# Gathered rows moved within the sample's attention, and a second gate load asked for later

## The reference

```python
x = layer_norm(x, emb_ln_g, emb_ln_b)
h = x @ w_in                                    # fourier, q, k, v, two gates
f_branch = fourier_mix(f_in) @ w_fo             # FFT over tokens and within groups of 64
a_branch = window_attention(q, k, v, sink) @ w_ao   # blocks of 128, neighbours, 8 heads, 2 kv heads
merged = gates[..., :D] * f_branch + gates[..., D:] * a_branch
x = layer_norm(alpha * x + merged @ w_out)
cm = peer(x, pq, pkeys, pu, pv)                 # 8 heads x 16 of 16384 experts per token
ple = sigmoid(x @ ple_wg) * (p @ ple_wp)
out = layer_norm(alpha * x + cm + ple)
# peer, per token: 128 experts chosen by product keys, gate = softmax of their scores
act = gelu(xc . u[eidx]);  cm = sum over k of gate_k * act_k * v[eidx_k]
```

## Time and profile before

| | |
|---|---|
| median of 3 runs | 3372.86 us (3372.45 to 3387.92) |
| the profiled execution | 3368.09 us |
| its span, first to last instruction | 3366.2 us |
| PE busy | 3206.8 us, 95% |
| PE weight loads busy | 2632.9 us, 78% |
| VectorE busy | 1968.2 us, 58% |
| GpSimd busy | 1866.5 us, 55% |
| ScalarE busy | 1024.1 us, 30% |
| moved by DMA | 988.38 MB, mean 294 GB/s |
| mean granted clock of TensorE | 0.982 of full |

### The profile page before, as it was taken

The page is one execution under the profiler, slowest core; times in us unless marked ns, Lnnn a source line. Parts: engine busy times, 40 slices in busy tenths (PEclk is TensorE's granted clock), DMA queues, the critical chain, the costliest instruction groups (busy, mean ns, idle before and its releaser), DMA issues.

```text
span 3366.2 us, 40493 instructions
## 1 busy us (share of the span) xinstructions
PE 3206.8 (95%) x14740; PEld 2632.9 (78%) x14740; DVE 1968.2 (58%) x3363; ACT 1024.1 (30%) x1427; POOL 1866.5 (55%) x1430
## 2 busy tenths in 40 slices
PE   7999899999999997899999999999997999999996
PEld 6677787888888886578778888888886888888885
DVE  3511315994100000854648997888885678887888
ACT  2432222333322221410102333444443223322231
POOL 3034344655544432665474332777777688888872
PEclk9999899999999999999999999999998999999998
DMA  6268678777777876598789998999999999999995
GB/s 243 91 213 274 225 243 301 242 241 240 243 238 244 252 242 226 149 347 336 257 320 350 317 326 293 371 393 394 393 394 409 353 340 340 343 354 333 346 349 180
DMA packets 322538, 988.38 MB, mean 294 GB/s; under 512 B 46896, under 2 KB 80176, under 8 KB 310960
## 3 DMA queue, kind: packets, MB, share of 16 engines
q1 hardware_dynamic: 226960, 708.80, 60.4%
q0 software_dynamic: 91264, 272.96, 22.6%
q10 hardware_dynamic: 4128, 4.19, 0.4%
HBM read 737.28 MB, written 248.51 MB: 293 GB/s over the span
## 4 chain that ended last, share of the span: by engine, by line
PE 55%; POOL 19%; issue 17%; DMA 3%; DVE 3%; another core or an unknown queue 2%; DVEq 1%; SPq 0%; ACT 0%; POOLq 0%; ACTq 0%
PE ps L1280 17%; PE ps L1282 17%; PE ps L1281 17%; POOL value L831 7%; POOL v_row L848 7%; POOL w_lo L797 4%; PE ps L1585 3%; POOL u_lo L797 1%; DMA v_row<-in_v_rows,row_i 1%; DVE acc L936 1%; DMA pair<-pair_dram 1%; DMA pair_dram<-w_lo 0%; PE ps L1503 0%; DMA u_lo<-lo_dram 0%
## 5 line engine op out<-in xcount | busy, mean ns | idle before, releaser
L1280 PE MATMUL ps<-xt_hi,w_hi 128*128 128x512 f32 (+1 forms) x2424 | 988.6, 408 | 32.0 <-issue 20.5
L848 POOL DMA_INDIRECT v_row<-in_v_rows,row_i x512 | 675.3, 1319 | 521.7 <-DVE acc L936 405.0
L1281 PE MATMUL ps<-xt_lo,w_hi 128*128 128x512 f32 (+1 forms) x2424 | 940.4, 388 | 0.0
L936 DVE SCALAR_TENSOR_TENSOR acc<-v_row,share,acc 128x1024 f32<-128x1024 f32 x512 | 658.0, 1285 | 249.7 <-DMA v_row<-in_v_rows,row_i 194.8
L1282 PE MATMUL ps<-xt_hi,u_lo 128*128 128x512 f32 x2048 | 801.4, 391 | 0.0
L831 POOL DMA_INDIRECT value<-act_dram,value_i x512 | 645.6, 1261 | 226.0 <-issue 155.7
L797 POOL TENSOR_TENSOR u_lo<-u_raw,w_hi 128x512 fp32r<-128x512 f32 x256 | 359.9, 1428 | 346.1 <-ACT w_hi L683 338.8
L1280 PEld LDWEIGHTS ps<-xt_hi,w_hi 128*128 128x128 f32 x2424 | 459.9, 190 | 110.7 <-issue 26.0
L1281 PEld LDWEIGHTS ps<-xt_lo,w_hi 128*128 128x128 f32 x2424 | 459.9, 190 | 71.2 <-issue 0.2
L1282 PEld LDWEIGHTS ps<-xt_hi,u_lo 128*128 128x128 f32 x2048 | 385.5, 188 | 82.4
L702 ACT ACTIVATE act_t<-ps 128x512 f32<-128x512 f32 x256 | 153.1, 598 | 971.9 <-PE ps L1282 888.2
(11 more groups left out here) (210 smaller groups left out, 4086.0 us busy)
## 6 DMA issues: line engine op xcount, KB each, us to landing
u_raw<-in_u_t SPq DMA_DIRECT2D x256, 512.0 KB
pair<-pair_dram SPq DMA_DIRECT2D x69, 1024.0 KB
lo_dram<-u_lo SPq DMA_DIRECT2D x128, 512.0 KB, 5.3
act_dram<-act_t SPq DMA_DIRECT2D x256, 256.0 KB
u_lo<-lo_dram SPq DMA_DIRECT2D x128, 512.0 KB
u_raw<-in_v_rows SPq DMA_DIRECT2D x128, 512.0 KB
w_raw<-in_weights SPq DMA_DIRECT2D x69, 512.0 KB, 5.2
pair_dram<-w_hi SPq DMA_DIRECT2D x69, 512.0 KB, 5.7
```

The lines of the kernel that those rows point to most:

```text
L848: pool.indirect_dma_start(out=v_row[:, i % ROWS_DEEP, :], out_offset=None, in_=v_rows, in_offset=bass.IndirectOffsetOnAxis(ap=row_i[:, tt, ...
L936: dve.scalar_tensor_tensor(out=there, in0=v_row[:, i % ROWS_DEEP, :], scalar=share[:, tt, k:k + 1], in1=there, op0=ALU.mult, op1=ALU.add). ...
L1280: pe.matmul(where, lh, rh, start=first, stop=False)
L1281: pe.matmul(where, lh, rl, start=False, stop=False)
```

## The change

Three things are changed. The rows added in the sample's attention: none in units 0 and 1, four in each of units 2 to 7 (24 in all, as before). The call with START_ROWS, which added nothing, is gone. And ScalarE asks for gate group 0 after the activation of tile 121 as before, and for group 1 after that of tile 126.

```diff
--- before.py
+++ after.py
@@ -74,7 +74,7 @@
 
 GATHERS = NT * HK
 ROWS_DEEP = 4
-START_ROWS, UNIT_ROWS = 0, 3
+UNIT_ROWS, ROWS_FROM = 4, 2
 GAP_ROWS, GAPS = 1, 10
 BATCH_ROWS, LAST_ROWS = 2, 18
 FIRST_VALUES = 18
@@ -85,7 +85,7 @@
 def rows_before(j):
 
     tiles = min(j, OUT_AT) - MERGE_AT + max(0, j - QUERY_AT)
-    return START_ROWS + UNITS * UNIT_ROWS + 2 * tiles
+    return (UNITS - ROWS_FROM) * UNIT_ROWS + 2 * tiles
 
 
 def reloaded(n):
@@ -134,7 +134,7 @@
     return ROWS_CHOICE + BATCH_ROWS * max(0, batch - 1)
 
 
-assert SEQS == 2 and FIRST_LOADS_AT + DEEP < EXPERT_TILES and EXPERT_TILES % DEEP == 0
+assert SEQS == 2 and FIRST_LOADS_AT + 5 < EXPERT_TILES and EXPERT_TILES % DEEP == 0
 
 
 def nth_norm(s, which):
@@ -750,11 +750,11 @@
                     if n == EXPERT_TILES - 1:
                         split_v(0)
                     gelu(n)
-                    if n == FIRST_LOADS_AT:
+                    if n in (FIRST_LOADS_AT, FIRST_LOADS_AT + 5):
                         act.wait_ge(g_stored, 16 * PIECES)
-                        for group in range(2):
-                            rows = slice(group * G_GROUP, (group + 1) * G_GROUP)
-                            act.dma_start(g_in[group][:], g_dram[:, :, rows, :].rearrange("c j i t -> j c i t")).then_inc(g_back[group], 16)
+                        group = (n - FIRST_LOADS_AT) // 5
+                        rows = slice(group * G_GROUP, (group + 1) * G_GROUP)
+                        act.dma_start(g_in[group][:], g_dram[:, :, rows, :].rearrange("c j i t -> j c i t")).then_inc(g_back[group], 16)
                     if n == NORM_PROMPT_AT:
                         deviation(4, prompt_norms)
                         prompt_norms += 1
@@ -1099,8 +1099,6 @@
                                           ps[rows, 3, :].rearrange("p (a b q) -> p a b q", a=2, b=2)[:, :, half, :],
                                           o_hi0[rows, 2 * g:2 * g + 2, cols_of(blk)].bitcast(F32), ALU.subtract).then_inc(o_lo_made, 1)
 
-                if s:
-                    add_rows(START_ROWS)
                 dve.wait_ge(mix_in, 32 * (s + 1))
                 scores(0)
                 dve.wait_ge(v_ps, s + 1)
@@ -1112,7 +1110,7 @@
                         outputs_lo(u - 1)
                     if u + 1 < UNITS:
                         scores(u + 1)
-                    if s:
+                    if s and u >= ROWS_FROM:
                         add_rows(UNIT_ROWS)
                     if u % 2 and s == 0:
                         c = u // 2
```

## The result

The changed kernel took 3395.49 us (median of 14 runs, 3383.31 to 3409.8); the kernel before, in 14 runs on the same chip, 3382.32 (3368.69 to 3396.76). The ratio is 1.0041, with a 95% interval of 1.0024 to 1.0058: about 14 us slower by the ratio, where a gain of 0.9 was forecast.

The account below looks back on a forecast made before the run. TensorE, busy 95% of 3366.2 us, was taken as the bound, VectorE setting its pace in attention units 2 to 5. +5.1 and -5.8 summed to -0.7 us, 3367.4 profiled, 3372 as median; range 3357 to 3381.

Parts of the forecast that it names:

- Edit 1, +5.1: Sample's attention: moving the row additions to units 2 to 7 makes the attention end 5.1 us later.
- 5.52 + 0.93 - 1.3: Sample's attention: 5.52 us later in units 2, 3, 4 and 6, 0.93 in unit 5, 1.3 earlier in unit 1.
- the fourth row: Sample's attention: a fourth gathered row per unit arrives in time, by 0.9 us with three key tiles.
- Edit 2, -5.8: Gate stage: asking for the second gate group after tile 126 wins 5.8 us net.
- 8.5: End of gate stage: the down stage can begin 8.5 us earlier, at 2626.9 instead of 2635.36.
- 2.67 for a slow start: Start of down stage: TensorE, having idled 8 us, pays 2.67 us for a slow start.
- A: Gate stage: loads keep up once TensorE moves, all 20.9 us are won, total 3357; chance 0.18.
- four short waits: Gate stage: queue 1 needs 6.7 us a tile, so TensorE waits 1 to 2 before tiles 123, 125, 126, 127.
- C: Gate stage: the second issue still blocks, at tile 126, so moving it brings nothing, total 3378; chance 0.08.
- D: Attention: added rows fall into waits set by TensorE or ScalarE, -1.3 in place of +5.1, total 3366; chance 0.17.
- B: Attention: with four row buffers VectorE waits for fourth rows in units 3 to 7, 5.7 us more, total 3378; chance 0.12.
- theory G: Whole kernel, from the experiments: while GpSimd issues gathers without rest for over some 10 us, TensorE runs slow until it rests.

Follow-up runs that it names:

- paced burst: Kernel before, with the 18 first value gathers asked for three at a time behind each of six weight tiles: 3359.55 us, 0.9947.
- where the gathers rest: 39 value gathers spread in threes ahead of the attention, in the kernel before with moved rows only (3364.88 us, 0.9987) and in the changed kernel (3366.11, 0.9983).
- the rows alone: Kernel before with only the moved rows (none in units 0 and 1, four in 2 to 7), gate loads as before: 3400.9 us, 1.0058.
- the early burst: Kernel before, with the 18 first value gathers allowed behind the third tile of v weights instead of the tenth: 3377.91 us, 0.998.
- The runs with rests: Changed kernel with 18 first value gathers in threes behind six weight tiles (0.9964), or 39 in threes over 13 points ahead of the attention (0.9983).
- the combined runs: Kernel before with second gate group after tile 126, plus 18 value gathers in threes (3353.76 us, 0.9949) or 39 in threes (3356.05, 0.9948).
- the double burst: Kernel before, with 36 instead of 18 value gathers issued ahead of the rows, the same number in all: 3392.43 us, 1.0064.

## Why the prediction was wrong

**What bounds the kernel.** Right that PE's idle time is what can be won, and that 20.46 us hung on the second issue of line 757. Wrong in passing over the 20.03 us in the attention with the words "that the diff doesn't touch". It is a cost of the same GpSimd queue that edit 1 rearranges: with the burst paced it fell to 3.23. I read its releaser by name, where the "remote" wait of 22.93 on VectorE and the unbroken issues on GpSimd stood beside it.

**Edit 1, +5.1: the step that failed.** Its arithmetic holds. Unit 2's normalisation came early (units 1 and 2 are 8.97 us apart instead of 10.53), the units then are 11.6 us apart, and where the gathers rest the attention is longer by 5.9 and 4.9 us. But the sum "5.52 + 0.93 - 1.3" counted only VectorE. The step asked of the fourth row whether it arrives in time, and never what its issue does to others. From unit 1 to unit 7 the attention grew by 12.9 us (72.43 for 59.49) and by 11.6 in the rows alone, of which 6 to 7 are PE's lateness behind the issues.

I had also written that PE works "without a break" through the merges. In the changed kernel it doesn't: here is PE, with GpSimd issuing until 1548.5, and ScalarE's wait that ended 2.8 us later:

```profile
1542.15 0.40 PE L1279 MATMUL ps<-o_lo,pair 128*128 128x512 f32 x1 [0.92 <-issue]
1542.84 0.39 PE L1280 MATMUL ps<-o_hi,pair 128*128 128x512 f32 x1 [0.30 <-issue]
1543.54 0.40 PE L1278 MATMUL ps<-o_hi,pair 128*128 128x512 f32 x1 [0.31 <-issue]
```

```profile
1551.35 0.60 ACT L636 ACTIVATE sig<-ps 128x512 f32<-128x512 f32 x1 [15.75 <-remote]
```

One matmul each 0.7 us, where these run at 0.23. But that this belongs to edit 1 isn't shown. From the attention's last output to the first product of the merged branches (tile `m`) PE took 139.7 us before (1425.8 to 1565.5) and 159.6 in the changed kernel, yet 140.3 with the rows alone, and 149.2 with the early burst and the rows of before. So of the 19.6 us, give or take 6, that edit 1 cost in time, the attention shows 11.6, and the rest isn't placed.

The runs with rests give a rougher price. With the gathers paced ahead of the attention the edit cost 5 (0.9964 for 0.9949), with rests in it too 12 (0.9983 for 0.9948), each give or take 9. Both allow VectorE's 5 alone, but the second, in which the attention has its rests, allows the 19.6 as well. So it is the profiles of the attention, not these times, that show the loss shrinking where GpSimd rests (5.9 and 4.9 for 12.9 and 11.6).

**Edit 2, -5.8.** Right in mechanism, and timed at -7, give or take 6. In the profiles, from the last gate matmul to the first down matmul (starts), the six kernels with the old order and the values took 70.6 to 73.6 us, the six with the new order 64.5 to 67.3: 6.3 less by the means, where I had 8.5. The down stage itself took 3.7 more (mean 710.2 for 706.5), where I had 2.67 for a slow start. So the profiles leave 2.6 us of it, the time says 7, give or take 6, and the combined runs show nothing that can be told from 0: the size stays open.

By the Trainium skill, page Trainium Kernel Development and Optimization, section Key Constraints, spreading issues "only saves the sequencer's issue time". The runs agree as far as they go: 18 us of issue vanished from ScalarE's queue and at most 13 of time.

**Rivals.** A (-20.9 in the gate stage) is out: the four short waits came back where queue 1 said. C is out: 395 ns. D is out: VectorE's units are 11.6 apart. B, the slower one, had the right sign and the wrong mechanism: rows wait for their buffers, but what comes late is PE's result. Its price, +5.7, was near the lateness in the attention (6 to 7) by luck.

**The range.** Of the 23 us between the forecast 3372 and 3395.49, 9.5 are in the base: the kernel before, 3372.86 in three runs, has a median of 3382.32 in 14. The other 14 are the change's. The range held nothing for a stretch in which another engine's habits change, and 0.86 on "within 0.5%" was right only because the loss, 0.41%, stays below it.

**The better kernel.** Before with the paced burst is 0.5% faster than before (0.9947) and, by the two ratios, 0.9% faster than the changed one (1.0041), with 18 gathers placed elsewhere and nothing removed.

## What to carry to other kernels

When a change fills the rests of an engine that issues indirect DMAs, ask what the slower pace was worth to TensorE, and look for waits laid to "remote" whose producer's row ends long before. Issue such gathers a few at a time behind events of the stream, not as one burst. And a large wait beside the change deserves its own reading, even where the diff doesn't name its line.

## What the runs showed of the hardware that I had not expected

GpSimd's indirect DMAs, one per 1.25 us without a rest, slowed TensorE here to a third or less. With the first burst it began some 13 to 20 us after the first of them. In the kernel before the results were there as the last gather was issued, elsewhere up to 5.7 us behind it, and in the double burst some came through in between (VectorE's at 1360.25, with GpSimd issuing until 1375.63). Ten us without a rest (1319.38 to 1329.1 with the paced burst) did nothing, and rests of up to 2 us behind each three prevented it. The onset, from PE's rows of the kernel with the early burst, whose GpSimd has issued since 1284.85:

```profile
1303.95 0.39 PE L1282 MATMUL ps<-xt_hi,pair 128*128 128x512 f32 x1
1304.72 0.39 PE L1280 MATMUL ps<-xt_hi,pair 128*128 128x512 f32 x1 [0.38 <-issue]
1306.14 0.39 PE L1281 MATMUL ps<-xt_lo,pair 128*128 128x512 f32 x1 [1.04 <-issue]
1307.55 0.40 PE L1282 MATMUL ps<-xt_hi,pair 128*128 128x512 f32 x1 [1.02 <-issue]
...
1310.37 0.59 PE L1281 MATMUL ps<-xt_lo,pair 128*128 128x512 f32 x1 [1.71 <-issue]
```

```profile
1304.00:1306.00 2.00, 0.73 (x3) 0.33 (x2) 0.00 (x0) 0.00 (x0) 1.63 (x2) 1.00 0.02 1
```

These matmuls follow one another at 0.23 us until 1303.95, then with gaps of up to 1.71 that are laid to nothing but "issue". It isn't the clock: in the stretch shown (columns as above) the granted clock is 1.00, the full 2.4 GHz, the first three matmuls behind gaps last 0.39 to 0.40 us as before them, and only the one at 1310.37 is longer, after PE has stood more than half the time. Nor is it bandwidth: the DMA share there is 0.02, as in a stretch of the kernel before in which the gathers run:

```profile
1328.00:1336.00 8.00, 1.27 (x6) 0.76 (x5) 0.00 (x0) 4.27 (x10) 6.17 (x7) 0.88 0.02 0
```

PE is busy for 1.27 of these 8 us. In the double burst the DMA engines moved 0.02 MB in all from 1334 to 1360, inside VectorE's wait of 31.30.

But unbroken issuing alone doesn't do it: theory G, as I put it above, is too broad. In the merges single gathers last up to 1.9 us, and two stretches of 36 gathers, first of the kernel before, then of the changed one, went differently:

```profile
1526.00:1580.00 54.00, 54.00 (x239) 44.69 (x239) 29.83 (x31) 5.83 (x9) 42.45 (x36) 1.00 0.96 358
```

```profile
1498.00:1548.00 50.00, 44.50 (x182) 34.00 (x181) 27.23 (x27) 3.55 (x6) 38.92 (x36) 0.96 0.90 332
```

In neither does GpSimd rest for more than 0.58 us, but the first has a gather each 1.50 us and PE is busy all the time; the second has one each 1.39, and PE stands for 5.5 of the 50 us. From 1240 to 1640 the thirteen kernels together have 33 stretches of over 20 us without a rest beyond 1 us. The 20 with a wait laid to "remote" in them or just behind have on average one gather per 1.28 to 1.43 us, the 13 without one per 1.42 to 1.52, the longest being 72 gathers in 109.8 us. The down stage fits too (177 in the 300 us from 2700 on in the kernel before, one per 1.69, and no such wait). So the lateness goes with the pace, and rests matter as they lower it. This is read from the profiles; no run changed the pace alone. What links the two engines inside the chip is open: no run here tells apart a shared path of instructions, of semaphores or of memory, nor GpSimd's work for a gather from the gather's own small transfers.
